# Six places in a two-block transformer kernel where the order of steps, or the place of a wait, is changed

## The reference, cut to what matters

```python
# first block: expert choice, 16 experts of 128 tokens each
a = jnp.einsum("becd,edf->becf", xin, w_gate)
b = jnp.einsum("becd,edf->becf", xin, w_up)
y = jnp.einsum("becf,efd->becd", jax.nn.silu(a) * b, w_down)
...
# second block
proj = h @ w_in[layer]
(glu_a, glu_b, z_conv, q, k, v, z_att, g_conv, g_att) = jnp.split(proj, split_idx, axis=-1)
u = glu_a * jax.nn.sigmoid(glu_b)
u = conv31(u)                                   # depthwise, 31 taps
u = jax.nn.silu(_layernorm(u, conv_ln_g[layer], conv_ln_b[layer]))
y_conv = (u * jax.nn.silu(z_conv)) @ w_conv_out[layer]
for gi, (window, dilation) in enumerate(DILATION_GROUPS):   # 3 groups of 8 heads
    o_g, m_g, d_g = _dilated_window_group(q[:, :, sl], k[:, :, sl], v[:, :, sl], window, dilation)
y_att = (att * jax.nn.silu(z_att)) @ w_att_out[layer]
merged = jax.nn.sigmoid(g_conv) * y_conv + jax.nn.sigmoid(g_att) * y_att
x = x + gate * (merged @ w_o[layer])
```

## Time and profile before

| | us |
|---|---|
| median of 3 runs | 2953.01 (2952.91 to 2954.65) |
| the profiled execution | 2951.67 |
| its span | 2949.8 |

### The profile page before, as it was taken

How to read it: one execution, slowest core, us unless ns; L and a number is a source line. 1 busy time by engine, 2 the same in 40 slices (tenths; PEclk the granted TensorE clock), 3 DMA queues, 4 the chain that set the end, 5 groups by cost and what they waited for, 6 DMA issues and landing times.

```text
span 2949.8 us, 36077 instructions
## 1 busy us (share of the span) xinstructions
PE 2811.1 (95%) x14332; PEld 2316.1 (79%) x14332; DVE 1780.6 (60%) x2497; ACT 1246.4 (42%) x2010; POOL 462.2 (16%) x423
## 2 busy tenths in 40 slices
PE   8999999899998899999995999999999999999998
PEld 6878888778885588888874787878878868588888
DVE  3644788330434788888884677777777764110554
ACT  4233787141321477777766124454454342011101
POOL 1400132000001211121104000000000163132231
PEclk9999999999998999999997999999999999999999
DMA  4120000421213999999984121030120221010131
GB/s 135 70 104 25 30 1 1 157 86 39 84 44 140 362 385 395 396 396 390 397 319 143 51 93 54 23 111 26 54 70 26 95 65 61 25 58 29 46 141 58
DMA packets 141459, 382.27 MB, mean 130 GB/s; under 512 B 11743, under 2 KB 45025, under 8 KB 141164
## 3 DMA queue, kind: packets, MB, share of 16 engines
q1 hardware_dynamic: 125036, 324.17, 29.1%
q0 software_dynamic: 13520, 46.28, 5.0%
q10 hardware_dynamic: 2736, 9.50, 0.9%
HBM read 340.47 MB, written 39.46 MB: 129 GB/s over the span
## 4 chain that ended last, share of the span: by engine, by line
PE 87%; DVE 7%; ACT 3%; issue 2%; DMA 1%; POOL 1%; SPq 0%; POOLq 0%; ACTq 0%; DVEq 0%
PE ps L2687 7%; PE ps L2688 7%; PE ps L2689 7%; PE ps L2330 6%; PE ps L2672 6%; PE ps L2674 6%; PE ps L2673 6%; PE ps L2344 5%; PE ps L2746 2%; PE ps L2748 2%; PE ps L2747 2%; PE ps L2789 2%; PE ps L2758 2%; PE ps L2760 2%; PE ps L2759 2%
## 5 line engine op out<-in xcount | busy, mean ns | idle before, releaser
L2110 DVE SCALAR_TENSOR_TENSOR b_f<-b_f,small_f 128x1023 f32<-128x1023 f32 (+14 forms) x240 | 304.3, 1268 | 69.5 <-ACT small_f L1209 40.9
L2687 PE MATMUL ps<-x_f32r,w_f32r 128*128 128x512 f32 x480 | 188.3, 392 | 0.8 <-issue 0.8
L2689 PE MATMUL ps<-x_f32r,w_f32r 128*128 128x512 f32 x480 | 187.1, 390 | 0.0
L2673 PE MATMUL ps<-w_f32r,a_f32r 128*128 128x512 f32 x456 | 178.0, 390 | 0.0
L2688 PE MATMUL ps<-ht_f32r,w_f32r 128*128 128x512 f32 x416 | 162.1, 390 | 0.0
L2747 PE MATMUL ps<-w_f32r,a_f32r 128*128 128x512 f32 x384 | 150.7, 392 | 0.0
L2330 PE MATMUL ps<-small_f 128*128 128x128 f32 (+1 forms) x632 | 89.3, 287 | 49.6 <-DVE small_f L1748 29.2
L2687 PE MATMUL ps<-ht_f32r,w_f32r 128*128 128x512 f32 x320 | 126.9, 397 | 9.4 <-issue 4.8
L2689 PE MATMUL ps<-ht_f32r,w_f32r 128*128 128x512 f32 x320 | 126.0, 394 | 0.0
L2673 PE MATMUL ps<-x_f32r,a_f32r 128*128 128x512 f32 x312 | 122.5, 393 | 0.0
L2330 PEld LDWEIGHTS ps<-small_f 128*128 128x128 f32 (+1 forms) x632 | 75.6, 144 | 59.6 <-DVE small_f L1748 31.5
(11 more groups left out here) (498 smaller groups left out, 7945.7 us busy)
## 6 DMA issues: line engine op xcount, KB each, us to landing
w_f<-in_w_exp_up SPq DMA_DIRECT2D x40, 1024.0 KB, 9.5
w_f<-in_w_exp_down SPq DMA_DIRECT2D x38, 1024.0 KB, 7.7
w_f<-in_w_exp_gate SPq DMA_DIRECT2D x36, 1024.0 KB, 7.9
x_f<-in_w_exp_gate SPq DMA_DIRECT2D x28, 1024.0 KB, 8.0
x_f<-in_w_exp_down SPq DMA_DIRECT2D x26, 1024.0 KB, 8.1
x_f<-in_w_exp_up SPq DMA_DIRECT2D x24, 1024.0 KB, 9.4
w_f<-in_w_in SPq DMA_DIRECT2D x22, 1024.0 KB, 5.1
w_f<-in_w_in SPq DMA_DIRECT2D x10, 2048.0 KB, 7.9
```

The source lines that it names most:

```text
L2110: ins = v.scalar_tensor_tensor(C_conv[k][:, d:S], U_conv[k][:, 0:S - d], cols[:, k, R_TAP + j:R_TAP + j + 1], C_conv[k][:, d:S], ALU.mult, ...
L2673: mm(o, x1, w2[:, k, c], start=False, stop=False)
L2687: mm(o, l1, r1, start=(k == 0), stop=False)
L2689: ins = mm(o, l2, r1, start=False, stop=(k == n - 1))
```

## The change

1. Last expert: the order g(15), d(14), u(15), d(15) becomes g(15), u(15), d(14), d(15). The hidden part of expert 15 is formed at d(14)'s first unit, and its transposes are placed in front of d(14)'s third.
2. First dilated tile: ScalarE's hi part is written right after the k weights are rounded, instead of behind the last `glu_a`; VectorE's lo copy is placed right behind the subtraction of the k weights, in front of the last `glu_a` multiply.
3. The two group changes (tiles 8 and 16): the v projection is moved behind values 0 and 1 and turns 2 and 3 of the tile before.
4. LayerNorm: `ht_rest(4)` follows the scales of tiles 1 to 4 instead of 0 to 3, the split of `gt3` that of tile 5 instead of 4.
5. Output product: token tiles 0 to 3 wait for `tmp_used` = 31, tile 4 for 32.

```diff
             for e in range(1, NE):
-                out += [("g", e), ("d", e - 1), ("u", e)]
+                out += [("g", e)] + ([("d", e - 1), ("u", e)] if e + 1 < NE else [("u", e), ("d", e - 1)])
...
-        HID_AT = {(unit["g", e + 1, 0] if e + 1 < NE else unit["d", e, 0]): e for e in range(NE)}
-        TURN_AT = {(unit["g", e + 1, 2] if e + 1 < NE else unit["d", e, 0]): e for e in range(NE)}
+        HID_AT = {(unit["g", e + 1, 0] if e + 1 < NE else unit["d", e - 1, 0]): e for e in range(NE)}
+        TURN_AT = {(unit["g", e + 1, 2] if e + 1 < NE else unit["d", e - 1, 2]): e for e in range(NE)}
...
+                fresh = new and i > 0 and tiles2[i][1] == 0
...
-                if new:
+                if new and not fresh:
                     yield "v", i, 0
                 if a >= 0:
                     for kd, u in (("values", 0), ("values", 1), ("turn", 2), ("turn", 3)):
                         yield kd, a, u
+                if fresh:
+                    yield "v", i, 0
...
-                if t < 4:
+                if 1 <= t < 5:
                     ht_rest(4)
-                elif t == 4:
+                elif t == 5:
                     split("gt3")
...
                     split_hi("k", GORDER[0])
+                    bk.read(act, ("glu_a", 3, 1, 0))
+                    nc.scalar.activation(tile_parts[0][0], value(group_tokens(*tiles2[0], src=HT_r)), ACT.Copy).then_inc(sem("tile_hi"), 1)
...
             bk.read(act, ("glu_a", 3, 1, 1))
-            nc.scalar.activation(tile_parts[0][0], value(group_tokens(*tiles2[0], src=HT_r)), ACT.Copy).then_inc(sem("tile_hi"), 1)
-            bk.read(act, ("glu_a", 3, 1, 0))
             chunk_out(7, U[7])
...
                         split_lo("qk"[pos // 2], GORDER[0])
+                        if pos == 2:
+                            v.tensor_copy(tile_parts[0][1], value(group_tokens(*tiles2[0], src=HT_Xr))).then_inc(sem("tile_lo"), 1)
...
-            bk.read(dve, ("glu_a", 3, 1, 1))
-            v.tensor_copy(tile_parts[0][1], value(group_tokens(*tiles2[0], src=HT_Xr))).then_inc(sem("tile_lo"), 1)
+            bk.wait(dve, ("glu_a", 3, 1, 1))
             dve.wait_ge(sem("tile_hi"), 1)
+            dve.wait_ge(sem("tile_lo"), 1)
...
-                    if j == 0 and t == 0:
-                        pe.wait_ge(sem("tmp_used"), 32)
+                    if j == 0 and t % 4 == 0:
+                        pe.wait_ge(sem("tmp_used"), 31 + t // 4)
```

## The result

The changed kernel takes 2971.37 us (median of 5; 2967.15 to 2972.22) against 2953.01 (2951.45 to 2956.71): ratio 1.0057, 95% interval 1.0042 to 1.0071, so it is slower by 0.6%. Its profiled execution took 2970.01 us with a span of 2968.2, 18.4 more than the 2949.8 before. The prediction was 2966.5 with a range of 2957 to 2974: the direction and the range held, the sum (+13.6) was 4.8 short.

The account below looks back on a forecast made before the run. TensorE, 87% of the chain, was taken to bound the kernel. 1.5 - 0.7 + 4.8 + 4.6 + 6.3 - 2.9 = +13.6 on the profiled 2951.67 gave 2965.3, for a median 2966.5; range 2957 to 2974 us.

Parts of the forecast that it names:

- Last expert, +1.5: At the last expert, a 4.4 us gap before d(15) plus some 0.9 for transposes, against 3.8 before: 1.5 us lost.
- each takes about 2 us against 2.7 of TensorE's, so they keep pace: At the last expert, ScalarE's roundings of d(15)'s other three units and write of y(14) were held not to delay TensorE.
- The gap of 4.4: At the last expert, 4.4 us from d(14)'s end to d(15), through hidden product, rounding and VectorE's first subtraction.
- First tile, -0.7: At the first dilated tile, q starts 2.1 us earlier, but qkt then waits for the rotation: 0.7 us gained.
- Group changes, +4.8 and +4.6: At tiles 8 and 16, turns 2 and 3 wait for exponentials behind VectorE's v subtractions: next q 4.8 and 4.6 us later.
- Rival (3): Group changes cost waiting only, v at full clock: +2.3 and +2.9, 2962.3 us; chance 0.15.
- Rival (1): At the group changes, maxima precede the v subtractions, so waits and slow stretches go: -11.4, 2945.8 us; chance 0.07.
- LayerNorm, +6.3: In the LayerNorm, scale 1 comes earlier, but gate products wait for late `ht_lo`: +5.5, plus 0.8 for the clock.
- The sign that I named: In the LayerNorm, two waits in front of the gate products at line 2687, released by GpSimd's line 1178.
- Output product, -2.9: At the output product, the wait of 2.81 us goes, with 0.1 of restart: 2.9 us gained.
- (2): In the LayerNorm, gate products don't wait for `ht_lo`: -1.6 instead of +6.3, 2958.7 us; chance 0.12.
- (4): More clock falls, at the first tile and twice in the LayerNorm, longer at the last expert: up to +8, 2974; chance 0.09.

Follow-up runs that it names:

- groups_max: Kernel before with v behind values 1 and turn 3 at both group changes, VectorE's maxima of scores 2 and 3 ahead of its v subtractions: 2957.42 us, ratio 1.0016.
- v_early: Kernel before with v unmoved, VectorE's four subtractions for it ahead of the rotation, two convolution steps behind the maxima: 2944.47 us, ratio 0.9978.
- norm_alone: Kernel before with only the LayerNorm edit, GpSimd's sixteen subtractions behind scales 1 to 4 and gt3's split behind scale 5: 2959.41 us, ratio 1.0021.
- last_two_hid: Kernel before with the last expert's new order, a second pair of hidden buffers and d(15) in PSUM banks 0 and 1: 2949.42 us, ratio 0.9992.

## Why the prediction was right, point by point

- *Last expert, +1.5; it was +3.4.* The wrong step is "each takes about 2 us against 2.7 of TensorE's, so they keep pace". That is true of the roundings; but the write of y(14), third in ScalarE's queue, frees the banks that d(15) begins in. The wait that the code has there was not read: it never showed before, since u(15) lay between d(14) and d(15). The gap of 4.4 was right (4.36 with other banks), and the missing 1.9 is 6.26 - 4.36. That the scatter of expert 14 comes later costs nothing.
- *First tile, -0.7; it was -0.9* (-1.0 alone). q at 1785.90 - 5.08 = 1780.8 for 1781.07, rotation 1805.36 - 5.08 = 1800.3 for 1800.44. The clock fell there before and didn't after.
- *Group changes, +4.8 and +4.6; it was +5.0 and +6.0, and +3.9 and +5.4 alone.* The mechanism was the one named: exponential 3 ended at 1980.19 - 4.24 = 1975.95 for 1975.94, and at 2178.46 - 9.26 = 2169.20 for 2169.22. v started at 1976.85 for 1976.4. At the second, v started 1.7 later than I had it: values 1 and turns 2 and 3 (1.97 and 1.91 us for 1.10 and 1.03 in front of the wait) themselves ran at the lower clock, and the sum had the clock on v only. That the totals came so close is partly luck: v behind this wait was priced at the 7.92 us of the shorter one, and took 7.70, 6.92 and 6.51 in the three profiles that have it. Rival (3), waiting only, fell: v ran at 0.70 to 0.88. Rival (1) fell because exponential 3 ended at 1975.95 and not before 1970.3. What its condition would give stays open, since `groups_max` reached only 1971.40 (+0.5); `v_early` (-10.7) shows that about that gain was there by another edit.
- *LayerNorm, +6.3; it was +6.2* (+6.9 alone). First wait over at 2419.30 - 15.29 = 2404.0 for 2403.9, eight subtractions at 2408.8 for 2408.8, sixteen at 2429.3 for 2428.7. One clock fall more was priced at 0.8; behind za4 it cost 1.6 (8.16 us for 6.55), but the wait in front of za6 takes that up, apart from 0.6 that made scale 4 late. The sign that I named, a release by GpSimd's line 1178, is not in the profile, which says "issue"; the ends of the batches stand for it.
- *Output product, -2.9; it was -3.1.* No wait, no later one. That the clock hadn't fallen there before is chance: it did in five of nine profiles with this wait.
- *The other rivals.* (2) fell: the gate products did wait for `ht_lo`, 2.98 and 2.48 us. (4) came true only in part: the clock fell longer in the LayerNorm and on values and turns at the second group change, but not at the first tile, and at the last expert as long as before (12.65 us for d(15), 12.67 before).
- *Left over:* 1.64 for the landing of the sum, which no part of the change makes. So of the 4.8 that the sum was short, 1.9 are a wait overlooked, 1.6 chance, 1.6 the clock around the group changes, and the rest cancels.

A row beside it: VectorE's shift of 128x512 took 4.27 us here beside GpSimd's split of `gt3` (from 2450.74, 4.58 us), 4.93 before, and 2.66 in `norm_alone` beside one from 2434.44 of 4.59.

```profile
2450.74 4.58 POOL L1128 TENSOR_TENSOR w_f32r<-w_f,w_f32r 128x2048 fp32r<-128x2048 f32 x1
...
2451.61 4.27 DVE L2280 TENSOR_TENSOR b_f<-b_f,small_f 128x512 f32<-128x512 f32 x1
```

It ends at 2455.88, 0.56 behind GpSimd's end at 2455.32; in `norm_alone` (2436.92 + 2.66 against 2439.03) and before (2423.42 + 4.93 against 2427.80) 0.55 behind it. However late it starts, it ends half a microsecond behind GpSimd. The Trainium skill (SBUF — State Buffer, Who interferes with whom) says that the second of the two to issue blocks until the first is done; the trace agrees. Beside GpSimd's short subtractions the price is small: four shifts from 2406.70 on in the kernel before took 0.82 to 1.07 us, and one at 2433.56 in the changed kernel, with GpSimd idle, 0.69.

## What to carry to other kernels

Moving work into a wait pays only if its own operands don't stand in the queue that makes the wait: read the releaser's queue first, and move that engine's work (-10.7 here) rather than the waiting engine's (+9 to +11). When two blocks become neighbours that never were, list every wait of the second one, PSUM banks and single buffers among them, though none shows in the trace. Price a wait as idle time plus a stretch at the lower clock, anything from nothing to 2.5 us on 24 matmuls here, and don't expect that stretch to shrink with the wait: in the kernels here it went only where the wait went, or was filled.

## What the runs showed of the hardware

- The slow stretch behind a wait doesn't follow the wait's length. d(15) took 12.67 us behind 1.78, 12.65 behind 6.26 and 13.58 behind 4.36; 24 matmuls of v took 7.92 behind 4.25 and 7.70 and 6.51 behind 8.0. At the first group change `groups_max` cut the wait from 8.0 to 3.41, and v's 24 matmuls still took 6.50. Where the wait went altogether (`last_two_hid`) or nearly (`v_early`, 0.51 left), so did the slow stretch.
- Matmuls whose result is never read hold the granted clock at 1.00, the 2.4 GHz level, through a wait of 4.25 us, and cost nothing if they end with it.
- The same wait may cost nothing or a fall. Behind 2.81 us in front of the output product, with the same code on every engine there, the next 48 matmuls took 5.98 to 5.99 us in four profiles and 7.23 to 8.65 in five (the clock of the next 6 us: 1.00 in the four, 0.50 to 0.76 in the five). One profile per kernel can mistake this for an effect of an edit hundreds of microseconds away.
- From the end of d(15) to the first work on the sum read back took 18.30 to 20.45 us in 13 profiles in which nothing of it was changed. A place's gain or loss has to be read between landmarks of one trace: the spread of 2.15 us is larger than what the first tile or the batches gave.
